# Carrying one stream of weight halves through the time mixer, the pool projections and the merge

## The chip, the core and the metric

The kernel runs on one core of a Trainium2 chip. The metric is the device time of one execution in microseconds (us), from three runs of the kernel before. The engines are TensorE (PE, with its weight loads PEld), VectorE (DVE), ScalarE (ACT), GpSimd (POOL) and SyncE (SP, which here issues transfers).

## What is computed

One decoder block: a layer norm over 272 tokens (16 of them prepended), two token mixers side by side, a gated merge, an output projection with layer norm, and a mixture of 16,384 experts with layer norm. The part that the change touches, cut from the reference:

```python
p = h @ w_in                                   # h: 272 x 2048; columns: r, k, v, low-rank parts, pool, two gates
ya = rwkv7_branch(p_rwkv, ...)                 # time mixer: 16 head pairs, delta rule over the tokens
yb = pool_branch(p_pool, w_pool, pool_scale)   # 4 groups of 256 columns, causal means over 2, 4, 8, 16 tokens minus the token,
                                               # then a 256 x 256 product per group
gate = sigmoid(p_gate + b_gate)
merged = gate[0] * (ya @ w_branch_a) + gate[1] * (yb @ w_branch_b)
h = layer_norm(ALPHA * h + merged @ w_out, ...)
h = layer_norm(ALPHA * h + peer_ffn(h, ...), ...)
```

Products that need float32 accuracy are made of three fp32r products: each operand is split into leading bits ("high") and the difference ("rest"), and high x high, high x rest and rest x high are added in PSUM.

## The kernel before

The stages run one behind the other, each in a block of its own that all engines leave together: input, low-rank projections, time mixer (rwkv_stage), pool_stage, merge_stage, out_stage, and the expert stage.

**Weights.** A weight tile of 128 columns has 16 k-tiles of 128 rows and comes in two halves of 8 k-tiles (128 x 1024 floats, 512 KB). A half is loaded by SP, its high part is made by a copy to fp32r, its rest by a subtraction on VectorE, and TensorE then does 24 products with it (8 k-tiles, three products each, in `product`, line 128).

**Time mixer.** 16 head pairs p go through a software pipeline of steps b = -1 to 18, written out by hand in ORDER: each entry is a name and an index, and STAGE gives by how many steps an entry lags (p = b - stage). `schedule` walks the list for every engine and calls that engine's function of the name where 0 <= p < 16. Entry "f" n does the next n k-tiles of the projections r, k, v of pair b on TensorE; "e" i moves a projected tile from PSUM (ScalarE line 597, then VectorE line 689); "sp" u and "ahead" round half u on ScalarE (line 586) and subtract on VectorE (line 113 through `rest_bits`). There are 48 "f" k-tiles in a step. Stage 1 (kn, lw, la, lg, ex, nm, bo, ab) makes decays, norms and keys, stage 2 (gr, rb, rk, Z, W, t) inverts the chunk matrices, stage 3 (r, u, s, yc, gm, gv, ge) runs the chain over five chunks and the group norm. So steps 16, 17 and 18 empty the pipeline: 16 has stages 1 to 3, 17 has stages 2 and 3, 18 has stage 3 alone, and none of them has an "f". "ge" on VectorE ends a pair: reciprocal (line 787), scale, bonus, and the product with the gate into `yaT` (line 794, semaphore `done`). Then "e" 2 follows, then the next step's first entries: "sp" 1, "cv", and "gr", where VectorE masks the Gram products (LT_st, line 732), on which TensorE's "rb" waits.

**Pool stage.** Four groups; SP loads 1 MB halves of 256 columns into one raw buffer (line 864) and the four 256 x 256 matrices `pool_mix` (line 867). VectorE makes high and rest of each (lines 108 and 113). TensorE does the projections `pool_u`, ScalarE copies them, VectorE adds shifted copies up to the window with a copy back after each doubling (lines 921 to 931), TensorE multiplies by `pool_mix` in plain float32 (line 876), ScalarE and VectorE make ybT_high and ybT.

**Merge stage.** 16 column tiles m, seven halves each: two gates, branch a (two halves each) and branch b (one half). Two buffers each for raw, high and rest. VectorE makes high (line 108) and rest (line 113); SP loads a half as soon as the split of the half two before it is done. At the start VectorE also splits all of `yaT` (128 x 4096). ScalarE does the sigmoids, VectorE the products, the sum and its split (`finish`, `keep`). The first and the last pass are written out, the others are a loop of the hardware over pairs of tiles. The first two transfers of `w_out` start after the first pass's loads.

Of the kernel before, what the change touches and what calls it, by code (L numbers as in the profile page):

```python
# [75 lines left out]
class Core:  # L76
# [5 lines left out]
    def sem(self, name):  # L82
        s = self.nc.alloc_semaphore(name)
        self.sems.append(s)
        return s
# [10 lines left out]
    def ps(self, name, shape, ctx):  # L96
        return ctx.enter_context(self.nc.psum_tensor(name, shape, F32))

# [168 lines left out]
def lora_stage(k, w):  # L267

    nc = k.nc
    with ExitStack() as ctx:  # L270
# [29 lines left out]
        def _(act):  # L300
# [24 lines left out]
         "r": 3, "u": 3, "s": 3, "yc": 3, "gm": 3, "gv": 3, "ge": 3}  # L325


def rwkv_stage(k, w):

    nc = k.nc  # L330
    with ExitStack() as ctx:
# [5 lines left out]
        raw = three("w_in", [P, HK, P])  # L337
        wh, wt = three("w_in_high", [P, HK, P]), three("w_in_rest", [P, HK, P])
# [26 lines left out]
        names = ("w_in0", "w_in1", "w_in2", "high", "split", "lora_w", "project", "own", "shifted", "rm", "lora_mm", "sig", "csum", "exps",  # L365
# [3 lines left out]
                 "done", "zero", "rst")  # L369
# [36 lines left out]
        W = w["w_in"][0].rearrange("(k p) c -> p k c", p=P)  # L406
# [5 lines left out]
        def _(sp):  # L412
            for b in range(PAIRS):
                for u in range(6):
                    wait(sp, q["split"], b * 6 + u - 2)
                    sp.dma_start(raw[u % 3][:], W[:, u % 2 * HK:u % 2 * HK + HK, b * P + u // 2 * D:b * P + u // 2 * D + P]).then_inc(q[f"w_in{u % 3}"], 16)
# [12 lines left out]
        def _(pe):  # L429
            at = [0]  # L430

            def f(n, b, par):

                for _ in range(n):
                    i, kt = divmod(at[0], KT)
                    u, kh = divmod(at[0], HK)
                    if kt == 0:
                        wait(pe, q["shifted"], b * 3 + i - 1)
                    if kh == 0:
                        wait(pe, q["split"], b * 6 + u + 1)  # L440
                    mm = product(nc, pr[(3 * par + i) % 2][:, 0:T], (wh[u % 3][:, kh, :], wt[u % 3][:, kh, :]),
                                 (k.hT_high[:, kt, :], k.hT[:, kt, :]), kt == 0, kt == KT - 1)
                    if kh == HK - 1:
                        mm.then_inc(q["project"], 1)
                    at[0] = (at[0] + 1) % (3 * KT)
# [135 lines left out]
        def _(act):  # L581
            def sp_(u, b, par):

                wait(act, q["project"], b * 6 + u - 2)
                wait(act, q[f"w_in{u % 3}"], b * 32 + 16 * (u // 3) + 16)
                nc.scalar.copy(wh[u % 3][:].bitcast(F32R), raw[u % 3][:]).then_inc(q["high"], 1)  # L586

            def e(i, p, par):

                o = (V_OMR, V_OMK, V_OMV)[i]  # L590
# [5 lines left out]
                wait(act, q["project"], p * 6 + 2 * i + 2)  # L596
                nc.scalar.activation(t[:, real], pr[(3 * par + i) % 2][:, 0:T], ACT.Copy, scale=cur[par][:, o:o + 1]).then_inc(q["own"], 1)
# [65 lines left out]
            def gv(_, p, par):  # L663
# [3 lines left out]

            wait(act, q["zero"], n_zero)
            schedule({"ahead": sp_, "sp": sp_, "e": e, "kn": kn_, "lw": lw, "la": la, "lg": lg, "ex": ex, "nm": nm, "ab": ab, "t": t, "r": r_, "u": u_,
                      "yc": y, "gm": gm, "gv": gv})  # L670

        @block.vector
        def _(dve):
            d, n = nc.vector.drain, nc.vector

            def sp_(u, b, par):

                wait(dve, q["high"], b * 6 + u + 1)
                rest_bits(nc.vector, wt[u % 3][:], raw[u % 3][:], wh[u % 3][:]).then_inc(q["split"], 1)
# [5 lines left out]
            def e(i, p, par):  # L685
                m = (V_MUR, V_MUK, V_MUV)[i]
                t = (r, kx, v)[i][par][:, PAD + 1:]
                wait(dve, q["own"], p * 3 + i + 1)
                n.scalar_tensor_tensor(out=t, in0=pr[(3 * par + i) % 2][:, 0:T - 1], scalar=cur[par][:, m:m + 1], in1=t,
# [95 lines left out]
            def ge(_, p, par):  # L785
# [8 lines left out]
                n.tensor_tensor(k.yaT[:, p, :], yc[:], gate[p % 3][:], ALU.mult).then_inc(q["done"], 1)  # L794
# [3 lines left out]
                      "Z": Z, "W": W_, "r": r_, "s": s_, "gm": gm, "ge": ge})  # L798
# [39 lines left out]
def pool_stage(k, w):  # L838

    nc = k.nc  # L840
    groups, gd = len(POOL_WINDOWS), POOL_DIM // len(POOL_WINDOWS)
    gt = gd // P
    with ExitStack() as ctx:
        HK = KT // 2
        raw = k.sb("pool_weights", [P, KT, gd], ctx=ctx)
        wh, wt = ([k.sb(f"pool_weights{n}{i}", [P, KT, gd], ctx=ctx) for i in range(2)] for n in ("_high", "_rest"))
        wm = k.sb("pool_mix", [P, groups, gt, gd], ctx=ctx)
        uu = k.sb("pool_in", [P, 2, gt, T], ctx=ctx)
        sm = k.sb("pool_sums", [P, 2, gt, T], ctx=ctx)
        pd = k.sb("pooled", [P, 2, gt, SEQ], ctx=ctx)  # L850
        pu = [[k.ps(f"pool_u{i}{j}", [P, 512], ctx) for j in range(gt)] for i in range(2)]
        pm = [[k.ps(f"pool_m{i}{j}", [P, 512], ctx) for j in range(gt)] for i in range(2)]
        s_w, s_wm = [k.sem("pool_w0"), k.sem("pool_w1")], k.sem("pool_wm")
        s_split, s_rest = k.sem("pool_split"), k.sem("pool_rest")
        s_u, s_uc, s_pd, s_m, s_y = k.sem("pool_u"), k.sem("pool_uc"), k.sem("pool_d"), k.sem("pool_m"), k.sem("pool_y")
        src = w["w_in"][0].rearrange("(k p) c -> p k c", p=P)
        block = ctx.enter_context(nc.Block())

        @block.sync
        def _(sp):  # L860
            for g in range(groups):
                for h in range(2):
                    wait(sp, s_split, 2 * (g - 1) + h + 1)
                    sp.dma_start(raw[:, h * HK:(h + 1) * HK], src[:, h * HK:(h + 1) * HK, POOL0 + g * gd:POOL0 + (g + 1) * gd]).then_inc(s_w[h], 16)
                if g == 0:
                    for h in range(groups):
                        sp.dma_start(wm[:, h, :, :], w["w_pool"][0, h].rearrange("(j p) d -> p j d", p=P)).then_inc(s_wm, 16)

        @block.tensor
        def _(pe):  # L870
            def mix(g):
                wait(pe, s_pd, g + 1)
                wait(pe, s_rest, gt * (g - 1))
                for j in range(gt):
                    for i in range(gt):
                        mm = nc.tensor.matmul(pm[g % 2][j][:, 0:SEQ], wm[:, g, i, j * P:(j + 1) * P], pd[:, g % 2, i, :],
                                              start=(i == 0), stop=(i == gt - 1))
                    mm.then_inc(s_m, 1)

            for g in range(groups):  # L880
                wait(pe, s_uc, gt * (g - 1))
                for j in range(gt):
                    for kt in range(KT):
                        if j == 0 and kt % HK == 0:
                            wait(pe, s_split, 2 * g + kt // HK + 1)
                        mm = product(nc, pu[g % 2][j][:, 0:T], [x[g % 2][:, kt, j * P:(j + 1) * P] for x in (wh, wt)],
# [725 lines left out]
```

## Time and profile before

| | us |
|---|---|
| three runs, median (lowest to highest) | 2838.03 (2835.0 to 2839.47) |
| the profiled execution: its time | 2838.6 |
| its span, first to last instruction | 2836.2 |
| time mixer, steps 16 to 18 (TensorE's part) | 80.7 |
| pool stage | 76.7 |
| merge stage | 369.7 |

Of the span TensorE is busy 81%, VectorE 59%, ScalarE 16%. The expert stage after 1400 us is bound by its gathers and doesn't depend on when it starts. All times within the trace count from the first instruction. A busy TensorE is not a TensorE at its peak: its products are pipelined and each record is longer than the distance to the next one.

### The profile page before, as it was taken

Reading aid. Unit: us, or ns where it says so; the run is one execution under the profiler, and the core shown is the slowest. Engines: PE = TensorE matmul, PEld = TensorE weight load, DVE = VectorE, ACT = ScalarE, POOL = GpSimd, SP = SyncE. Lnnn points to the kernel's source line nnn. Section 1 sums busy time; section 2 is a strip of 40 time slices with the busy share of each in tenths; the row PEclk is TensorE's granted clock in tenths of the full one; section 3 lists DMA queues with packets and bytes.
Section 4 is the critical chain, followed back from the end, with each engine's and each line's share of the span. In section 5 each row is a group of like instructions: output and inputs, shape, how many; then the busy total and the mean of one; then the engine's idle time right before and its main releaser. Section 6 shows DMA issues by size and latency. Waiting matters only on the chain.

```text
span 2836.2 us, 42516 instructions
## 1 busy us (share of the span) xinstructions
PE 2286.5 (81%) x17604; PEld 1614.7 (57%) x17604; DVE 1668.3 (59%) x2643; ACT 459.0 (16%) x1043; POOL 654.1 (23%) x541
## 2 busy tenths in 40 slices
PE   4899998989867799999778778878777777777776
PEld 3788888888857799997663334433223223222222
DVE  6466666666655666666655565456644634444444
ACT  1443343334320000000010111011100100000000
POOL 1000000000000000000035335435554535444442
PEclk9999999999988899999889889889999999999999
DMA  3532323232104556564479999989999999999996
GB/s 123 134 82 72 81 66 83 64 83 69 49 2 134 155 165 169 166 167 156 153 259 407 376 376 407 403 347 420 420 420 420 421 384 410 420 420 420 420 420 272
DMA packets 354342, 710.17 MB, mean 250 GB/s; under 512 B 13656, under 2 KB 278256, under 8 KB 287600
## 3 DMA queue, kind: packets, MB, share of 16 engines
q0 software_dynamic: 74176, 537.01, 46.0%
q1 hardware_dynamic: 280000, 170.78, 21.1%
q8 instruction: 124, 2.03, 0.3%
q14 instruction: 42, 0.34, 0.0%
HBM read 705.64 MB, written 2.10 MB: 250 GB/s over the span
## 4 chain that ended last, share of the span: by engine, by line
DMA 27%; PE 13%; DVE 6%; issue 2%; DVEq 1%; POOL 1%; ACT 0%; ACTq 0%
DMA down_rows<-in_v_table,experts 22%; PE peer_sum L1358 6%; DMA up_rows<-in_u_table,experts 5%; PE query_then_peer_sum L1358 5%; PE query_then_peer_sum L1321 2%; DVE up_rows L1495 2%; POOL down_rows L1303 0%; POOL up_rows L1296 0%; DVE expert_sides L1477 0%; DVE side_index L1439 0%; DVE side_index L1446 0%; DVE one_hot L1475 0%; DVE scores_left L1440 0%; DVE top_pos L1446 0%; DVE top_pos L1439 0%
## 5 line engine op out<-in xcount | busy, mean ns | idle before, releaser
L1495 DVE CUSTOM_DVE_ANT_0 up_rows<-up_rows,h 128x2048 f32<-128x2048 f32 x256 | 585.5, 2292 | 624.6 <-DMA up_rows<-in_u_table,experts 624.6
L1296 POOL DMA_INDIRECT up_rows<-in_u_table,experts x256 | 271.6, 1061 | 1463.6 <-DVE experts L1481 1370.9
L1358 PE MATMUL query_then_peer_sum<-down_rows,diagonal 128*128 128x512 f32 x1024 | 472.9, 607 | 157.5 <-DMA down_rows<-in_v_table,experts 108.7
L1358 PE MATMUL peer_sum<-down_rows,diagonal 128*128 128x512 f32 x1024 | 476.0, 608 | 98.6 <-DMA down_rows<-in_v_table,experts 95.0
L1303 POOL DMA_INDIRECT down_rows<-in_v_table,experts x256 | 374.0, 1461 | 613.9 <-PE peer_sum L1358 316.5
L1358 PEld LDWEIGHTS query_then_peer_sum<-down_rows,diagonal 128*128 128x128 f32 x1024 | 186.3, 191 | 444.0 <-DMA down_rows<-in_v_table,experts 240.0
L1358 PEld LDWEIGHTS peer_sum<-down_rows,diagonal 128*128 128x128 f32 x1024 | 191.3, 193 | 340.2 <-issue 188.4
L128 PE MATMUL project<-hT_high,w_in_high 128*128 128x272 f32 x768 | 246.1, 320 | 11.1 <-DVE w_in_rest L113 11.1
L128 PE MATMUL project<-hT_high,w_in_rest 128*128 128x272 f32 x768 | 223.0, 290 | 0.0
L128 PE MATMUL project<-hT,w_in_high 128*128 128x272 f32 x768 | 222.4, 290 | 0.0
L1415 ACT ACTIVATE dots<-dots 128x4 f32<-128x4 f32 x64 | 13.1, 205 | 997.4 <-DVE dots L1495 997.4
L113 DVE TENSOR_TENSOR w_in_rest<-w_in,w_in_high 128x1024 fp32r<-128x1024 f32 x96 | 117.2, 1220 | 91.4 <-ACT w_in_high L586 91.4
L128 PE MATMUL merge_ps<-hT_high,merge_w_high 128*128 128x256 f32 x512 | 152.0, 297 | 22.9 <-DVE merge_w_rest L113 21.9
L128 PEld LDWEIGHTS project<-hT_high,w_in_high 128*128 128x128 f32 x768 | 145.8, 190 | 17.1 <-DVE w_in_rest L113 11.3
L128 PEld LDWEIGHTS project<-hT,w_in_high 128*128 128x128 f32 x768 | 146.1, 190 | 3.8
L128 PE MATMUL merge_ps<-hT,merge_w_high 128*128 128x256 f32 x512 | 146.2, 285 | 0.0
L128 PE MATMUL merge_ps<-hT_high,merge_w_rest 128*128 128x256 f32 x512 | 146.1, 285 | 0.0
L128 PEld LDWEIGHTS project<-hT_high,w_in_rest 128*128 128x128 f32 x768 | 145.8, 190 | 0.0
L113 DVE TENSOR_TENSOR merge_w_rest<-merge_w,merge_w_high 128x1024 fp32r<-128x1024 f32 x112 | 137.3, 1226 | 8.3
L108 DVE CAST merge_w_high<-merge_w 128x1024 fp32r<-128x1024 f32 x112 | 77.6, 693 | 102.5 <-DMA merge_w<-in_w_in 46.5
L128 PEld LDWEIGHTS merge_ps<-hT_high,merge_w_high 128*128 128x128 f32 x512 | 99.3, 194 | 33.3 <-DVE merge_w_rest L113 32.8
L586 ACT CAST w_in_high<-w_in 128x1024 fp32r<-128x1024 f32 x96 | 100.1, 1043 | 10.5 <-DMA w_in<-in_w_in 6.0
(308 smaller groups left out, 3665.7 us busy)
## 6 DMA issues: line engine op xcount, KB each, us to landing
w_in<-in_w_in SPq DMA_DIRECT2D x96, 512.0 KB, 4.4
merge_w<-in_w_in SPq DMA_DIRECT2D x64, 512.0 KB, 4.0
merge_w<-in_w_branch_a SPq DMA_DIRECT2D x32, 512.0 KB, 3.9
out_w<-in_w_out SPq DMA_DIRECT2D x16, 1024.0 KB, 5.1
pool_weights<-in_w_in SPq DMA_DIRECT2D x8, 1024.0 KB, 5.4
merge_w<-in_w_branch_b SPq DMA_DIRECT2D x16, 512.0 KB, 3.9
out_w<-in_w_q_peer SPq DMA_DIRECT2D x8, 1024.0 KB, 17.4
query_w<-in_w_q_peer SPq DMA_DIRECT2D x8, 1024.0 KB, 28.2
```

The costliest lines, as they stand in the source:

```text
L108: return nc.vector.tensor_copy(high.bitcast(F32R), x)
L113: return eng.tensor_tensor(low.bitcast(F32R), x, high, ALU.subtract)
L128: mm = nc.tensor.matmul(out, a.bitcast(F32R), b.bitcast(F32R), start=start and n == 0, stop=stop and n == 2)
L586: nc.scalar.copy(wh[u % 3][:].bitcast(F32R), raw[u % 3][:]).then_inc(q["high"], 1)
L1296: pool.indirect_dma_start(ur[n % RU][:], None, w["u_table"][0], bass.IndirectOffsetOnAxis(ap=k.idx[:, t, h, j:j + 1], axis=0)).then_inc(s_ ...
L1303: pool.indirect_dma_start(vr[n % RV][:], None, w["v_table"][0], bass.IndirectOffsetOnAxis(ap=k.idx[:, t, h, j:j + 1], axis=0)).then_inc(s_ ...
L1321: mm = nc.tensor.matmul(pq[i][:, 0:SEQ], wt[h % 2][i][:, kt, :], k.h1T[:, kt, :], start=(kt == 0), stop=(kt == KT - 1))
L1358: mm = nc.tensor.matmul(acc[t][c][:], dg[n % RD][:], vr[n % RV][:, c * 512:(c + 1) * 512], start=False, stop=(n % (HEADS * TOPK) == HEADS ...
L1415: nc.scalar.activation(x, x, ACT.Gelu).then_inc(s_gelu, 1)
L1495: v.tensor_tensor_reduce(ur[n % RU][:], ur[n % RU][:], k.h[:, n // (HEADS * TOPK), :], 1.0, 0.0, ALU.mult, ALU.add, dots[:, n:n + 1]).then ...
```

## The change

A list `halves` holds all weight halves of the time mixer (96), of the pool projections (16) and of the merge (112) in the order of use. Three raw, three high and three rest buffers carry it, with semaphores that live through both stages. `load_half`, `round_half` (ScalarE) and `rest_half` (VectorE) treat every half alike. Pool projections: the "f" entries of steps 16 to 18 do the eight pool tiles (128 k-tiles: 48, 48 and 32), "e" copies them on VectorE into `pool_in`. The last entries of step 18 round the first three merge halves. "ge" leaves y in `yc`; ScalarE copies it into `ya_high`, and a new entry "gy" at the end of the list subtracts on VectorE into `ya_rest`, so that the split of all of `yaT` is gone. `pool_stage` is gone: its window sums (without the copies back) stand in the first two slots of VectorE's merge, its mix between the gate products and the branch a product of tile m = 0. The merge is fully written out, with rounding on ScalarE.

Its core:

```diff
+    def load_half(self, sp, g):
+        src, h, c0 = self.halves[g]
+        wait(sp, self.s_split, g - 2)
+        sp.dma_start(self.w_raw[g % 3][:], src[:, h * KT // 2:(h + 1) * KT // 2, c0:c0 + P]).then_inc(self.s_raw[g % 3], 16)
+
+    def round_half(self, act, g):
+        wait(act, self.s_used, g - 2)
+        act.wait_ge(self.s_raw[g % 3], 16 * (g // 3) + 16)
+        self.nc.scalar.copy(self.w_high[g % 3][:].bitcast(F32R), self.w_raw[g % 3][:]).then_inc(self.s_rounded, 1)
+
+    def rest_half(self, dve, g):
+        dve.wait_ge(self.s_rounded, g + 1)
+        rest_bits(self.nc.vector, self.w_rest[g % 3][:], self.w_raw[g % 3][:], self.w_high[g % 3][:]).then_inc(self.s_split, 1)
...
-    ("ab", 0), ("W", 5), ("gm", 0), ("f", 4), ("gv", 0), ("f", 4), ("ge", 0), ("e", 2),
+    ("ab", 0), ("W", 5), ("gm", 0), ("f", 4), ("gv", 0), ("f", 4), ("ge", 0), ("e", 2), ("gy", 0),
...
+STREAM = ("ahead", "sp", "f", "e")
...
-                    if name in units and 0 <= p < PAIRS:
+                    if name in units and 0 <= p < (PAIRS + 4 if name in STREAM else PAIRS):
...   # SP, end of the time mixer
+            for g in range(PAIRS * 6, k.merge_at + 3):
+                k.load_half(sp, g)
...   # VectorE, "e"
+                if p >= PAIRS:
+                    if tile < k.merge_at // 2:
+                        dve.wait_ge(k.s_used, 2 * tile + 2)
+                        n.tensor_copy(k.pool_in[:, tile - 3 * PAIRS, :], pr[tile % 2][:, 0:T]).then_inc(q["shifted"], 1)
+                    return
...   # ScalarE, between "gv" and "e" 2
+            def ge(_, p, par):
+                wait(act, q["y"], p + 1)
+                nc.scalar.copy(k.ya_high[:, p, :].bitcast(F32R), yc[:]).then_inc(q["yhigh"], 1)
...   # VectorE
-                n.tensor_tensor(k.yaT[:, p, :], yc[:], gate[p % 3][:], ALU.mult).then_inc(q["done"], 1)
+                n.tensor_tensor(yc[:], yc[:], gate[p % 3][:], ALU.mult).then_inc(q["y"], 1)
+            def gy(_, p, par):
+                wait(dve, q["yhigh"], p + 1)
+                rest_bits(n, k.ya_rest[:, p, :], yc[:], k.ya_high[:, p, :]).then_inc(q["done"], 1)
...   # merge_stage, SP
+            for g in range(groups):
+                sp.dma_start(wm[:, g, :, :], w["w_pool"][0, g].rearrange("(j p) d -> p j d", p=P)).then_inc(s_wm, 16)
+            for g in range(first + 3, last):
+                k.load_half(sp, g)
+                if g == first + 12:
...   # the two w_out transfers
...   # merge_stage, TensorE
+            for m in range(KT):
+                wait(pe, s_done, m - 1)
+                if m == 1:
+                    pe.wait_ge(s_yb, 2 * groups)
+                tile(m, 0, h)
+                tile(m, 1, h)
+                if m == 0:
+                    mix()
+                tile(m, 2, (k.ya_high, k.ya_rest))
+                if m == 0:
+                    pe.wait_ge(s_yb, 2 * groups)
+                tile(m, 3, (k.ybT_high, k.ybT))
...   # merge_stage, VectorE
+            for m in range(KT):
+                for j, (n, h) in enumerate(parts):
+                    g = first + m * PARTS + j
+                    if g + 3 < last:
+                        k.rest_half(dve, g + 3)
+                    if j == 0 and m:
+                        keep(m - 1)
+                    if m == 0 and j < 2:
+                        window(2 * j)
+                        window(2 * j + 1)
```

In the merge ScalarE's list is likewise: round half g + 3 at slot g, then at fixed slots the sigmoids, the copy of the last sum into `mT_high`, and (m = 0, slot 3) the eight copies into `ybT_high`.

## Rows read from the trace of the kernel before

**Rows 1.** Windows by stage: length; PE, PEld, DVE, ACT, POOL busy; clock; DMA

```profile
725.88:770.52 44.64, 41.43 (x702) 38.42 (x701) 30.23 (x61) 17.08 (x35) 0.00 (x0) 1.00 0.11 31
770.52:804.05 33.53, 24.85 (x557) 20.43 (x556) 22.59 (x52) 10.77 (x27) 0.00 (x0) 0.93 0.01 2
804.05:828.93 24.88, 20.04 (x545) 18.12 (x545) 15.25 (x37) 4.78 (x16) 0.00 (x0) 0.95 0.01 3
828.93:851.20 22.27, 12.60 (x140) 9.01 (x140) 8.67 (x17) 3.39 (x13) 0.00 (x0) 0.53 0.00 1
851.20:927.90 76.70, 60.10 (x416) 57.87 (x416) 43.51 (x45) 6.89 (x16) 0.00 (x0) 0.86 0.41 124
927.90:1297.60 369.70, 344.89 (x2688) 329.76 (x2688) 251.10 (x325) 15.61 (x33) 0.00 (x0) 0.97 0.59 165
```

**Rows 2.** Timeline of VectorE: the same instruction of steps 4 and 15

```profile
224.92 0.17 DVE L730 COPY chunk_decay<-decay_prod 128x5 f32<-128x5 f32 x1
730.16 0.17 DVE L730 COPY chunk_decay<-decay_prod 128x5 f32<-128x5 f32 x1
```

**Rows 3.** Timeline, step 14 into 15: start, us, engine, line, operation, idle before it

```profile
725.99 0.49 ACT L597 ACTIVATE v<-project,pair_vectors 128x272 f32<-128x272 f32 x1 [0.98 <-PE project L128]
726.38 1.03 ACT L586 CAST w_in_high<-w_in 128x1024 fp32r<-128x1024 f32 x1
...
728.01 0.43 DVE L794 TENSOR_TENSOR yaT<-y,gate 128x256 f32<-128x256 f32 x1
728.35 0.49 DVE L689 SCALAR_TENSOR_TENSOR v<-project,pair_vectors,v 128x271 f32<-128x271 f32 x1
728.76 1.22 DVE L113 TENSOR_TENSOR w_in_rest<-w_in,w_in_high 128x1024 fp32r<-128x1024 f32 x1
...
730.23 0.49 DVE L732 TENSOR_TENSOR LT_st<-invert,constants 128x320 f32<-128x320 f32 x1
...
731.45 0.63 PE L387 MATMUL invert<-R_st,B_st 64*64 64x64 f32 x16
```

**Rows 4.** Timeline of TensorE: six k-tiles of projection to what follows; a chain wait

```profile
728.83 0.39 PE L128 MATMUL project<-hT_high,w_in_high 128*128 128x272 f32 x1
...
731.29 0.33 PE L387 MATMUL chain<-rhs,Y_st 64*64 64x64 f32 x4
...
836.93 0.48 PE L387 MATMUL chain<-BKV_by_token 64*64 64x64 f32 x4 [0.31 <-ACT U L652]
```

**Rows 5.** Tile pool_sums, one line of it: count, ns min/median/max, first and last

```profile
L925 DVE TENSOR_TENSOR pool_tmp<-pool_sums x6: 695/715/721, 890.4 to 920.7; 128x538 f32<-128x538 f32 x3, 128x530 f32<-128x530 f32 x2, 128x514 f32<-128x514 f32 x1
```

**Rows 6.** Timeline: start of the pool stage on SP, its end and the merge's start on TensorE

```profile
852.40 1.01 SPq L864 DMA_DIRECT2D pool_weights<-in_w_in  x2
853.46 4.30 SPq L867 DMA_DIRECT2D pool_mix<-in_w_pool  x4
...
923.08 3.78 PE L876 MATMUL pool_m<-pooled,pool_mix 128*128 128x256 f32 x8 [4.51 <-DVE pooled L931]
...
935.27 0.41 PE L128 MATMUL merge_ps<-hT_high,merge_w_high 128*128 128x256 f32 x1
...
939.12 0.41 PE L128 MATMUL merge_ps<-hT_high,merge_w_high 128*128 128x256 f32 x1
```

**Rows 7.** Tile merge_w_high; transfers with us to landing; two matmuls nine apart

```profile
L108 DVE CAST merge_w_high<-merge_w x112: 683/694/696, 932.4 to 1292.3; 128x1024 fp32r<-128x1024 f32 x112
L113 DVE TENSOR_TENSOR merge_w_rest<-merge_w,merge_w_high x112: 1224/1226/1228, 933.2 to 1293.0; 128x1024 fp32r<-128x1024 f32 x112
...
merge_w<-in_w_in SPq DMA_DIRECT2D x64, 512.0 KB, 4.0
...
pool_mix<-in_w_pool SPq DMA_DIRECT2D x4, 256.0 KB, 7.1
...
1107.19 0.28 PE L128 MATMUL merge_ps<-hT_high,merge_w_high 128*128 128x256 f32 x1
1108.25 0.28 PE L128 MATMUL merge_ps<-hT_high,merge_w_high 128*128 128x256 f32 x1
```

More of the change, by code:

```diff
@@ L676, in sp_ @@
             def sp_(u, b, par):
-                wait(dve, q["high"], b * 6 + u + 1)
-                rest_bits(nc.vector, wt[u % 3][:], raw[u % 3][:], wh[u % 3][:]).then_inc(q["split"], 1)
+                if b * 6 + u < k.merge_at + 3:
+                    k.rest_half(dve, b * 6 + u)
             def cv(_, p, par):
@@ L835, in row_broadcast, with merge_stage, mixed @@
     return v.rearrange("(a d) -> a d", a=1).to_broadcast((P, D))
-def pool_stage(k, w):
+def merge_stage(k, w):
     nc = k.nc
-    groups, gd = len(POOL_WINDOWS), POOL_DIM // len(POOL_WINDOWS)
-    gt = gd // P
+    groups = len(POOL_WINDOWS)
     with ExitStack() as ctx:
         HK = KT // 2
[L845 to L856, printed above, removed]
+        parts = [(n, h) for n, kts in enumerate((KT, KT, KT, KT // 2)) for h in range(kts // HK)]
+        PARTS = len(parts)
+        gt = [k.sb(f"merge_gates{i}", [P, 2, SEQ], ctx=ctx) for i in range(2)]
+        ps = [[k.ps(f"merge_ps{i}{n}", [P, 512], ctx) for n in range(4)] for i in range(2)]
+        wm, sums = k.pool_mix, k.pool_sums
+        s_wm, s_pd, s_mix = k.sem("pool_wm"), k.sem("pool_d"), k.sem("pool_mixed")
+        s_yb_high, s_yb = k.sem("pool_y_high"), k.sem("pool_y")
+        s_gate, s_sum, s_high, s_done = k.sem("merge_gate"), k.sem("merge_sum"), k.sem("merge_high"), k.sem("merge_done")
+        first, last = k.merge_at, k.merge_at + KT * PARTS
         block = ctx.enter_context(nc.Block())
+        def mixed(m):
+            return ps[1][m // 2][:, m % 2 * SEQ:m % 2 * SEQ + SEQ]
         @block.sync
@@ L869, in _ @@
+            for g in range(first + 3, last):
+                k.load_half(sp, g)
+                if g == first + 12:
+                    for i in range(2):
+                        sp.dma_start(k.out_raw[i][:], w["w_out"][0].rearrange("(k p) c -> p k c", p=P)[:, 4 * i:4 * i + 4, 0:512]).then_inc(k.s_out_w[i], 16)
         @block.tensor
         def _(pe):
[L871 to L886, printed above, removed]
-                                     (k.hT_high[:, kt, :], k.hT[:, kt, :]), kt == 0, kt == KT - 1)
-                    mm.then_inc(s_u, 1)
-                if g == 1:
-                    pe.wait_ge(s_wm, 16 * groups)
-                if g:
-                    mix(g - 1)
@@ L893, in _, with tile @@
-            mix(groups - 1)
+            def tile(m, n, xs):
+                hs = [j for j, (o, _) in enumerate(parts) if o == n]
+                for j in hs:
+                    g = first + m * PARTS + j
+                    pe.wait_ge(k.s_split, g + 1)
+                    for kh in range(HK):
+                        kt = parts[j][1] * HK + kh
+                        mm = product(nc, ps[m % 2][n][:, 0:SEQ], [x[g % 3][:, kh, :] for x in (k.w_high, k.w_rest)],
+                                     [x[:, kt, :] for x in xs], kt == 0, j == hs[-1] and kh == HK - 1)
+                    mm.then_inc(k.s_used, 1)
@@ new lines, in mix @@
+            def mix():
+                pe.wait_ge(s_wm, 16 * groups)
+                for g in range(groups):
+                    pe.wait_ge(s_pd, g + 1)
+                    for j in range(2):
+                        for i in range(2):
+                            mm = nc.tensor.matmul(mixed(2 * g + j), wm[:, g, i, j * P:(j + 1) * P], k.pool_in[:, 2 * g + i, META:T],
+                                                  start=(i == 0), stop=(i == 1))
+                        mm.then_inc(s_mix, 1)
@@ L1093, in out_stage @@
+            keep(KT - 1)
 def out_stage(k, w):
@@ L1573, in program @@
                 lora_stage(k, w)
+            k.open_weights(w, front)
+            k.ya_high, k.ya_rest = (k.sb(f"yaT_{n}", [P, KT, SEQ], ctx=front) for n in ("high", "rest"))
+            k.pool_in = k.sb("pool_in", [P, POOL_DIM // P, T], ctx=front)
             rwkv_stage(k, w)
```

301 lines of the change are left out of this document (99 added, 202 removed).

## The prediction, made before the change was run

> **What bounds the kernel now.** I read the windows by stage first [rows 1]. Their rows are the last full step of the time mixer (15), the emptying steps 16, 17 and 18, the pool stage and the merge, cut where TensorE starts each. In the full step TensorE is busy 41.43 of 44.64 us at full clock: it sets the pace. In the emptying steps it is busy 24.85 of 33.53, 20.04 of 24.88 and 12.60 of 22.27 us, the last at a granted clock of 0.53, near the lower of its two levels (1.2 and 2.4 GHz). There it waits for VectorE and ScalarE, and that time is free for other products. The pool stage is 76.70 us with 60.10 of TensorE. The merge is 369.70 us. Its work is 112 halves of 24 products; between two products of an undisturbed run lie (1108.25 - 1107.19) / 9 = 0.118 us [rows 7], so 2.83 us a half and 317 us in all. The other 53 us are waits and low clock, since two buffers make load, split and use wait for each other. Then I read single instructions in the timeline: the end of a step [rows 3], a chain wait [rows 4], and both ends of the pool stage [rows 6]. The stages before the time mixer and after the merge keep their work, and the expert stage moves as a whole with the end of the merge, so the sum covers the time from step 4 to the end of the merge.
>
> **The ends of the full steps (A).** New: ScalarE copies y into ya_high and VectorE subtracts (gy). The copy sits on ScalarE ahead of "e" 2 and "sp" 1, and waits for VectorE's product with the gate, which ends at 728.44; before, ScalarE did "e" 2 at 725.99 and the rounding at 726.38 [rows 3]. Queued behind that wait are "e" 2 (0.49), the rounding (1.03), and the next copies of the chain. The copy has no row; I take 0.4, between 0 and the 0.49 of "e" 2, which is longer by 16 columns. So "e" 2 ends on ScalarE near 729.25, on VectorE near 729.75 (before: 728.84), gy (as long as the 0.43 of line 794) near 730.1, the rounding near 730.2, its subtraction (1.22) near 731.45 instead of 729.98. Everything behind on VectorE is late by 1.45 us, LT_st too: it ends at 732.2 instead of 730.72. TensorE's "rb" waits for it and began at 731.45, so 0.7 of the 1.45 was slack, and 0.75 us is lost. Behind that, TensorE's own order covers VectorE's delay. Bounds: 0 (slack elsewhere) and 1.5 (all of it passes on). Twelve steps' ends (3 to 14) lie ahead of step 15: 12 x 0.75 = **+9.0** (0 to 18).
>
> **Steps 15 and 16 (B).** Step 16 now holds three pool tiles and is a full step again; its "e" is one VectorE copy instead of two moves, which I value at -0.2. A full step takes (730.16 - 224.92) / 11 = 45.93 us [rows 2]. New: 2 x (45.93 + 0.75) - 0.2 = 93.2; before 44.64 + 33.53 = 78.17. **+15.0.**
>
> **Step 17 (C).** Three more tiles. Six k-tiles take 731.29 - 728.83 = 2.46 us with their start [rows 4], four of them 1.70 by share of products. A step has six runs of 6 and three of 4: 19.86. With 20.04 us of other work that is 39.9 if every gap is filled and 44.7 if none is. In step 16 the same sum with all gaps filled is 24.85 + 19.86 = 44.7, and the measured full step has 1.2 more. Step 17 lacks the decays and norms that keep VectorE late, so I take half of that, and 0.75 for the end of step 16: 41.25 against 24.88, **+16.4** (15 to 20).
>
> **Step 18 (D).** Two tiles: five runs of 6 (12.3) and one of 2 (0.95). The runs stand between u and s of the chain and cover ScalarE's copy of U, 0.31 in each of five chunks [rows 4], so -1.55. With products between, the clock should stay up: of 12.60 us at the low level, some 8 lie ahead of the tail (the mean and variance products and their waits) and would take half: -4. The new copy and subtraction end the stage: +0.9. 22.27 + 13.25 - 1.55 - 4 + 0.9 = 30.9, **+8.6** (4 to 13, without cover and clock, or with S covered too). The roundings and subtractions of these steps are hidden under the runs; without that cover each costs 1.03 + 1.22.
>
> The time mixer ends 49 us later. **Pool stage:** -76.7.
>
> **Start of the merge (E).** From the time mixer's end at 851.20 to the first transfer behind it 1.2 us pass [rows 6], and stay. Three halves lie ready. The clock is low: 18 products take 939.12 - 935.27 = 3.85, so the first half takes 5.1, the next two 2.85 each: 10.8. The fourth, half 115, stands on SP behind the four loads of pool_mix, which took 4.30 to issue; with 4.0 to landing [rows 7], rounding and subtraction it is ready near 11.6. TensorE does it until 14.5. VectorE has done its subtraction at 11.6 and then does the window sums, which nothing hides: 1 + 2 + 3 + 4 additions and 4 combinations of some 0.72 [rows 5], 10.1, with the gaps between them I say 11 us, and the subtraction of 116 between them: 23.7. TensorE stands until then, its last mix at low clock takes 3.8 [rows 6], which gives 27.5 with the first groups' mix done in the wait. Then halves 116 (partly at low clock, 4.7), 117 and 118: **38 us** for m = 0 (31, if transfers and windows come earlier, to 44).
>
> **The other 15 tiles (F).** Rounding on ScalarE 1.03, subtraction 1.23, issue and landing about 4.4: 6.7 us for a raw buffer that comes round every three halves (8.6 us), and 2.3 us for a high buffer that is given back two halves before its next use is due. VectorE has 7 x 1.23 = 8.6 us of it a tile and ScalarE 7 x 1.03 = 7.2, with a few operations of 256 columns each, both not much over half of the 20 us. So TensorE is the bound: 2.83 + 0.04 for a half's first product (a guess), 105 x 2.87 = **301.4**. Upper bound: the old pace, 369.70 / 112 = 3.30 a half. A rule speaks against moving the rounding. VectorE rounded a half in 0.69 [rows 7] where ScalarE takes 1.03 [rows 3]. The Trainium skill ("ScalarE: Activation LUTs", Rules for kernel authors) wants simple elementwise work on VectorE, which it gives up to three times ScalarE's rate in bf16; the rows show 1.5 times here. By the rows the longer rounding lies under 5.7 us of other halves' products.
>
> **Sum.** Before, from 851.20 to the merge's end: 76.7 + 369.7 = 446.4. After, from the same point: 9.0 + 15.0 + 16.4 + 8.6 + 1.2 + 38 + 301.4 = 389.6. Gain 56.8, so 2838.6 - 56.8 = 2781.8 against the profiled execution, which stands 0.6 above the median of three runs; I say **2781**.
>
> **Rivals.** (1) VectorE's whole delay passes on at each of 14 ends of steps: 14 x 0.75 = 10.5 more, 2791.5. For it: TensorE waits for VectorE at several other places in a step. Against: it follows its own order for some 5 us behind "rb". (2) The ends of steps cost nothing and the runs fill every gap: A and B lose 10.5, C 1.4, D 4.6, so 2765. For it: step 16 shows how near filling comes. (3) The merge keeps its pace, that is, three buffers do not free TensorE: 105 x (3.30 - 2.87) = 45 more, 2826. Against: its waits begin with split and load, which get one more buffer. (4) Slower than before: the weights themselves. The raw ring gives one half per (0.4 + landing + 1.03 + 1.23) / 3. At a landing of 5.9 us it reaches TensorE's 2.87; the gain of 57 is gone at 3.41 a half, a landing of 7.6; at 8 us it is 3.55, 72 more, 2853. For it: pool_mix landed in 7.1 with several transfers queued [rows 7]. Against: 4.0 for the very transfers, at a DMA share of 0.59 [rows 1], which a pace of 2.87 lifts to about 0.68. (5) The rounding lies on the path: 112 x 0.34 = 38 more, 2820. It needs TensorE to use up its two ready halves. The rule on ScalarE above would make this the outcome; the trace so far speaks against it.
>
> **How the numbers follow.** Chances: the forecast 0.64, with its own range 2765 to 2797; rival 1 0.12, 2 0.10, 3 0.07, 4 0.04, 5 0.03. The range 2762 to 2804 takes in the forecast's, 1 and 2, and leaves out 3, 4 and 5 and some of the forecast's tails, about 2 in 10. A measurement of this kernel can tell about 0.2%, 5.7 us, from no change: only rival 4 isn't faster by that, and a landing between 7 and 7.6 us would be within. So faster 0.95, same 0.01, slower 0.04.
>
> **What would show it.** The copies of chunk_decay 46.7 us apart instead of 45.9 would bear out A, with a new wait of TensorE's "rb" for LT_st near 0.75. Step 17 near 41 and step 18 near 31 us at a clock above 0.8 bear out C and D. In the merge's first tile: a wait of some 9 us before the last mix. From the second tile on TensorE's windows at 2.87 a half with no waits for the subtraction; waits of ScalarE's rounding for a transfer would be rival 4. The prediction is wrong if projections in the emptying steps open new waits in the chain, or if the merge's pace isn't TensorE's.

## The result, and the profile after

| | before | after |
|---|---|---|
| median of 4 runs each, us | 2836.52 (2832.26 to 2839.47) | 2772.14 (2770.33 to 2773.89) |
| ratio, 95% interval | | 0.9774 [0.9757, 0.9791] |
| profiled execution, us (span) | 2838.6 (2836.2) | 2773.89 (2771.8) |
| end of the time mixer, us from the start | 851.20 | 900.18 |
| end of the merge | 1297.60 | 1235.2 |

The kernel became 64.4 us faster; the forecast was a gain of 56.8 and a time of 2781, in a range that holds the measured one. Run once more (k9_changed below), the same two kernels stood at 2773.72 and 2830.90, a gain of 57.2. So several us of a single difference belong to the run, and the steps below are read from traces, not from the totals.

The windows of the changed kernel, by stage, as [rows 1] has them for the kernel before (length; busy time of TensorE, its weight loads, VectorE, ScalarE, GpSimd; granted clock; DMA share; GB/s). They are step 17, step 18, the merge's start with its first tile, and its other 15 tiles:

```profile
828.36:867.00 38.64, 38.49 (x695) 36.34 (x695) 24.55 (x47) 10.30 (x22) 0.00 (x0) 1.00 0.31 84
867.00:900.20 33.20, 22.24 (x232) 19.01 (x230) 16.40 (x28) 9.68 (x21) 0.00 (x0) 0.88 0.18 48
900.20:935.40 35.20, 29.94 (x202) 28.24 (x203) 20.49 (x29) 11.56 (x18) 0.00 (x0) 0.92 0.56 150
935.40:1235.20 299.80, 299.80 (x2520) 299.75 (x2518) 147.67 (x163) 123.81 (x148) 0.00 (x0) 1.00 0.68 185
```

In the last row TensorE is busy all the time, at full clock: the merge has become TensorE's. In the row of step 17 it is busy 38.49 of 38.64 us, where step 17 of before stood for 4.84 of 24.88 [rows 1].

The waits in that last stretch (who waited, for whom: us in total, times, longest):

```profile
ACT w_half_high L124 <- PE merge_ps L160: 160.0, 97, 1.8
DVE w_half_rest L145 <- ACT w_half_high L124: 145.6, 103, 4.7
ACT w_half_high L124 <- DMA w_half<-in_w_in: 5.5, 4, 2.6
```

None of the waits in this stretch is TensorE's. ScalarE waits 97 times for TensorE to give a rounded buffer back, and only a few times for a transfer: the data are there before their place is.

The end of step 14 into 15, timeline of VectorE, ScalarE and TensorE (start, us, engine, line, operation, idle before it), to be laid beside [rows 3]:

```profile
737.56 0.43 DVE L837 TENSOR_TENSOR y<-y,gate 128x256 f32<-128x256 f32 x1
738.02 0.41 ACT L704 CAST yaT_high<-y 128x256 fp32r<-128x256 f32 x1 [3.46 <-DVE y L837]
738.33 0.48 ACT L631 ACTIVATE v<-project,pair_vectors 128x272 f32<-128x272 f32 x1
738.84 0.50 DVE L732 SCALAR_TENSOR_TENSOR v<-project,pair_vectors,v 128x271 f32<-128x271 f32 x1 [0.86 <-ACT v L631]
739.26 0.41 DVE L145 TENSOR_TENSOR yaT_rest<-y,yaT_high 128x256 fp32r<-128x256 f32 x1
739.78 1.23 DVE L145 TENSOR_TENSOR w_half_rest<-w_half,w_half_high 128x1024 fp32r<-128x1024 f32 x1
741.26 0.48 DVE L775 TENSOR_TENSOR LT_st<-invert,constants 128x320 f32<-128x320 f32 x1
741.89 0.68 PE L419 MATMUL invert<-R_st,B_st 64*64 64x64 f32 x16 [0.72 <-DVE LT_st L775]
```

ScalarE's copy stands ahead of its part of v, and waits 3.46 us for VectorE's product with the gate; v's second half on VectorE then waits 0.86 for ScalarE, and TensorE's R_st x B_st 0.72 for `LT_st`. Before, the same product followed without a wait [rows 3].

The same VectorE instruction of steps 4 and 15, as in [rows 2]:

```profile
226.84 0.16 DVE L773 COPY chunk_decay<-decay_prod 128x5 f32<-128x5 f32 x1
...
741.19 0.16 DVE L773 COPY chunk_decay<-decay_prod 128x5 f32<-128x5 f32 x1
```

Eleven steps take 514.35 us, 46.76 a step against 45.93.

Step 18, first chunk of the chain (timeline of ScalarE and TensorE):

```profile
868.96 0.40 ACT L704 CAST yaT_high<-y 128x256 fp32r<-128x256 f32 x1 [3.44 <-DVE y L837]
869.27 1.04 ACT L124 CAST w_half_high<-w_half 128x1024 fp32r<-128x1024 f32 x1
870.22 0.20 ACT L682 COPY rhs<-chain 128x64 f32<-128x64 f32 x1
870.48 0.33 PE L419 MATMUL chain<-rhs,Y_st 64*64 64x64 f32 x4 [1.30 <-ACT rhs L682]
871.54 0.33 PE L419 MATMUL chain<-BKV_by_token 64*64 64x64 f32 x4 [0.73 <-ACT U L686]
```

The chain's copy of `rhs` stands behind the copy of y and a rounding on ScalarE, and TensorE waits 1.30 and then 0.73 us.

The merge's start (SP, ScalarE, VectorE, TensorE), as [rows 6] for before:

```profile
901.49 3.34 SPq L910 DMA_DIRECT2D pool_mix<-in_w_pool  x4
910.15 1.05 ACT L124 CAST w_half_high<-w_half 128x1024 fp32r<-128x1024 f32 x1 [10.44 <-DMA w_half<-in_w_in]
912.51 0.39 PE L160 MATMUL merge_ps<-hT_high,w_half_high 128*128 128x256 f32 x1 [0.24 <-DVE w_half_rest L145]
915.43 3.62 PE L936 MATMUL merge_ps<-pool_in,pool_mix 128*128 128x256 f32 x16
920.80 1.99 PE L936 MATMUL merge_ps<-pool_in,pool_mix 128*128 128x256 f32 x8 [1.75 <-DVE pool_in L991]
923.98 0.69 DVE L991 SCALAR_TENSOR_TENSOR pool_in<-pool_sums,pool_in 128x512 f32<-128x512 f32 x1
924.73 1.99 PE L936 MATMUL merge_ps<-pool_in,pool_mix 128*128 128x256 f32 x8 [1.94 <-DVE pool_in L991]
```

### The profile page after: what moved, and what is told of

The parts are those of the page before. It is cut to its first block, busy times and chain, and to the rows that moved or that the text cites. A ratio compares the mean times of both kernels' runs of the same rounds, so it can differ in the third digit from the quotient of the medians.

```text
span 2771.8 us, 41744 instructions
## 1 busy us (share of the span) xinstructions
PE 2258.8 (81%) x17604; PEld 1602.2 (58%) x17604; DVE 1574.3 (57%) x2507; ACT 592.0 (21%) x1195; POOL 653.6 (24%) x541
## 4 chain that ended last, share of the span: by engine, by line
DMA 28%; PE 14%; DVE 6%; issue 2%; DVEq 1%; POOL 1%; ACT 0%; ACTq 0%
DMA down_rows<-in_v_table,experts 22%; PE peer_sum L1291 7%; DMA up_rows<-in_u_table,experts 5%; PE query_then_peer_sum L1291 5%; PE query_then_peer_sum L1254 2%; DVE up_rows L1428 2%; POOL down_rows L1236 0%; DVE expert_sides L1410 0%; POOL up_rows L1229 0%; DVE side_index L1379 0%; DVE side_index L1372 0%; DVE one_hot L1408 0%; DVE scores_left L1373 0%; DVE top_pos L1379 0%; DVE top_pos L1372 0%
## 5 line engine op out<-in xcount | busy, mean ns | idle before, releaser
L145 DVE TENSOR_TENSOR w_half_rest<-w_half,w_half_high 128x1024 fp32r<-128x1024 f32 x224 | 273.8, 1223 | 270.8 <-ACT w_half_high L124 269.4
L160 PE MATMUL project<-hT_high,w_half_high 128*128 128x272 f32 x896 | 286.9, 320 | 11.2 <-DVE w_half_rest L145 11.2
L124 ACT CAST w_half_high<-w_half 128x1024 fp32r<-128x1024 f32 x224 | 234.4, 1047 | 197.2 <-PE merge_ps L160 163.9
L160 PE MATMUL project<-hT_high,w_half_rest 128*128 128x272 f32 x896 | 260.4, 291 | 0.0
L160 PE MATMUL project<-hT,w_half_high 128*128 128x272 f32 x896 | 259.9, 290 | 0.0
L160 PEld LDWEIGHTS project<-hT_high,w_half_high 128*128 128x128 f32 x896 | 170.5, 190 | 18.6 <-DVE w_half_rest L145 11.4
L160 PEld LDWEIGHTS project<-hT,w_half_high 128*128 128x128 f32 x896 | 170.6, 190 | 4.1
L160 PEld LDWEIGHTS project<-hT_high,w_half_rest 128*128 128x128 f32 x896 | 170.4, 190 | 0.0
L160 PE MATMUL merge_ps<-hT,w_half_high 128*128 128x256 f32 x512 | 145.1, 283 | 0.0
L160 PE MATMUL merge_ps<-hT_high,w_half_rest 128*128 128x256 f32 x512 | 144.9, 283 | 0.0
## 6 DMA issues: line engine op xcount, KB each, us to landing
out_w<-in_w_q_peer SPq DMA_DIRECT2D x8, 1024.0 KB, 18.1
```

The costliest lines, as they stand in the source:

```text
L124: self.nc.scalar.copy(self.w_high[g % 3][:].bitcast(F32R), self.w_raw[g % 3][:]).then_inc(self.s_rounded, 1)
L145: return eng.tensor_tensor(low.bitcast(F32R), x, high, ALU.subtract)
L160: mm = nc.tensor.matmul(out, a.bitcast(F32R), b.bitcast(F32R), start=start and n == 0, stop=stop and n == 2)
```

## The experiments

My theory: the gain is what the pool tiles find free in the emptying steps, plus a merge that a third raw buffer makes TensorE's; the losses are the new copy at each step's end and the windows that stand open in the merge's first tile. The rivals are that another part of the change freed the merge (the third rounded buffer, or the rounding's move to ScalarE), and that the pool tiles' place is indifferent.

**Two raw buffers in the merge.** The load of a half waits for the split of the half two before it, not three before it as in the changed kernel, so that only two of the three raw buffers are in use.

```diff
-        wait(sp, self.s_split, g - 2)
+        wait(sp, self.s_split, g - 1 if g >= self.merge_at + 3 else g - 2)
```

> From half 115 on (the merge) a load waits one split longer, so that two raw buffers are in flight instead of three; high and rest keep three. Theory (the merge's old pace was set by the ring of raw buffers: load, round, subtract, with only two of them): a half then takes (0.4 issue + 4.0 landing + 1.05 rounding + 1.23 subtraction + hand-overs) / 2 = 3.35 to 3.4 us instead of 2.86, so the merge is some 55 us longer and the kernel near 2825; ScalarE's rounding waits for transfers in the trace. Rival (the pace came from the high and rest buffers, or from VectorE's rounding, and the third raw buffer adds nothing): 2772, within 5.

Measured: 2821.42 us, ratio to the kernel before 0.9962 [0.9946, 0.9978]. From the start of the first `ybT` half (931.9) to the end of the last (1286.3) lie 106 halves in 354.4 us, 3.34 us each; in the changed kernel the same takes 302.8, 2.857 each. The waits from 940 to 1280:

```profile
ACT w_half_high L124 <- DMA w_half<-in_w_in: 118.9, 56, 4.2
ACT w_half_high L124 <- DMA w_half<-in_w_branch_a: 59.0, 30, 4.4
...
PE merge_ps L160 <- DVE w_half_rest L145: 34.2, 51, 2.8
```

ScalarE now waits 178 us for those two transfers alone, and TensorE for the subtraction. With a landing of 4.1 us in this run, (0.4 + 4.1 + 1.05 + 1.23) / 2 = 3.39 us a half, close to the 3.34: the ring of loads sets the pace. The third raw buffer is worth 52 us of the changed kernel's merge; without it the kernel is 10.9 us faster than before.

The sum holds for the kernel before too: its 106 halves took 339.6 us (958.0 to 1297.6), 3.20 each, and with VectorE's 0.69 for the rounding (0.4 + 4.0 + 0.69 + 1.23) / 2 = 3.16. With two raw buffers the slower rounding on ScalarE thus made the ring slower, not faster. This kernel keeps the written-out merge and has no split of all of `yaT` either, so neither of these freed the merge.

**Two rounded buffers in the merge.** Rounding and subtraction of half g + 2 stand at slot g, and the rounding waits for the use of half g.

```diff
-        wait(act, self.s_used, g - 2)
+        wait(act, self.s_used, g - 1 if g >= self.merge_at + 3 else g - 2)
...
-                    if g + 3 < last:
-                        k.round_half(act, g + 3)
+                    if first + 3 <= g + 2 < last:
+                        k.round_half(act, g + 2)
```

(the same for the subtraction on VectorE)

> In the merge the rounding of a half comes one slot later and waits for the use of the half two before it, so that high and rest have two buffers in use; raw keeps three. Theory (only the raw ring set the old pace): after a half's use 1.05 + 1.23 and hand-overs are 2.4 us, under the 2.86 that TensorE spends on the half in between, so the pace stays at 2.86 and the time within 5 us of 2772, with at most some tenths of a us a tile where VectorE's products delay a subtraction. Rival (the third high and rest buffer frees TensorE): back to 3.1 to 3.3 a half, 2797 to 2820.

Measured: 2771.07 us, ratio 0.9783 [0.9767, 0.9800]. The part behind the first tile takes 305.1 us, 2.3 more than in the changed kernel; the first tile is 3 shorter, since VectorE comes to the windows sooner. The third rounded buffer gains next to nothing: it did not free the merge.

**VectorE rounds in the merge**, all three buffers as in the changed kernel.

```diff
-                    if g + 3 < last:
-                        k.round_half(act, g + 3)
...
-                        k.rest_half(dve, g + 3)
+                        x = (g + 3) % 3
+                        dve.wait_ge(k.s_used, g + 1)
+                        dve.wait_ge(k.s_raw[x], 16 * ((g + 3) // 3) + 16)
+                        split(nc, k.w_high[x][:], k.w_rest[x][:], k.w_raw[x][:]).then_inc(k.s_split, 1)
```

> In the merge VectorE rounds and subtracts, as before the change, with the stream's three buffers of each kind; ScalarE rounds only up to half 114. Theory (TensorE is the bound, whoever rounds): VectorE needs 7 x (0.69 + 1.23 + 0.08) + 1.7 = 15.7 us of the 20 a tile, so the pace stays at 2.86; the first tile may lose 1 to 3 us, since VectorE has the window sums there too: 2772 to 2776. Rival (moving the rounding to ScalarE was what freed the merge): 3.1 to 3.3 a half, 2797 to 2820. The rule that simple elementwise work belongs on VectorE would have it faster: 2765 or less.

Measured: 2777.76 us, ratio 0.9806 [0.9790, 0.9823], some us above what I expected, though the intervals of this ratio and the changed kernel's overlap. Its first tile is 2.9 us longer and the part behind it 303.8, 1.0 longer. Its waits:

```profile
DVE w_half_high L140 <- PE merge_ps L160: 60.5, 81, 0.9
DVE w_half_high L140 <- DMA w_half<-in_w_branch_b: 5.2, 1, 5.2
```

VectorE, too, waits for TensorE to give buffers back and not for data. With three raw buffers it hardly matters where the rounding stands; its move did not free the merge.

**The pool tiles behind step 18.** The projections of the eight pool tiles leave the emptying steps and run in one piece behind them.

```diff
-                        if name in units and 0 <= p < (PAIRS + 4 if name in STREAM else PAIRS):
+                        if name in units and 0 <= p < PAIRS:
...
+            f(POOL_DIM // P * KT, PAIRS, 0)
```

(and rounding, subtraction and the moves likewise in one run on their engines)

> The eight pool tiles stand behind step 18 in one run instead of in the runs of steps 16 to 18; the stream, its order and its buffers are the same. Theory (the emptying steps' gaps cover a part of the projections, and the rest of the pool stage's saving is the stream's: no load to wait for, no separate mix): steps 16 to 18 go back to some 81 us plus the new ends of steps, and the projections take 16 x 3.0 + 2.3 for the first split + 2.5 of low clock = 53 in a row, so the time mixer's end moves from 900 to some 918 and the kernel to 2790 (2786 to 2794). Rival (the cover is the whole gain of the part): 2772 + 40 or more.

Measured: 2793.49 us, ratio 0.9862 [0.9842, 0.9882]. The run of pool tiles:

```profile
867.30:923.50 56.20, 50.41 (x384) 50.22 (x384) 26.86 (x28) 19.38 (x19) 0.00 (x0) 0.95 0.56 150
```

It takes 56.2 us up to the merge's first product, where the pool stage of before took 76.70 [rows 1]: the stream of halves is loaded ahead, and the windows and the mix stand in the merge now, where they still take time. The merge's first product comes at 923.5 instead of 901.5: in the emptying steps the same tiles cost 22 us less, the free time of TensorE there. So the place of the tiles counts, and both rivals fall, mine and that the cover is the whole gain of the part.

**The copy of y later.** ScalarE's copy of y goes behind the key norms of the next step, VectorE's subtraction behind the second Z product; the list runs one step longer for the last pair, and nothing else moves.

```diff
-    ... ("t", 1), ("kn", 0), ("f", 6),
-    ("r", 1), ("Z", 1), ("u", 1), ("lw", 0), ...
+    ... ("t", 1), ("kn", 0), ("gc", 0), ("f", 6),
+    ("r", 1), ("Z", 1), ("u", 1), ("gy", 0), ("lw", 0), ...
-    ... ("ge", 0), ("e", 2), ("gy", 0),
+    ... ("ge", 0), ("e", 2),
-         ... "ge": 3, "gy": 3}
+         ... "ge": 3, "gc": 4, "gy": 4}
```

> ScalarE's copy of y into its high part and VectorE's subtraction leave the end of the step and stand in the next one: the copy behind the key norms, the subtraction behind the second Z product, where both engines wait. Theory (the copy holds up ScalarE's move of v, its rounding and so VectorE's masks, and TensorE's product R_st x B_st waits 0.72 us for them in every step): the wait is gone, copies of chunk_decay lie 45.8 to 46.0 us apart again instead of 46.7, 13 steps x 0.75 = 9.8 less, and up to 2 us in step 18 where the chain's first copies stood behind it: 2760 to 2763. Rival (any place costs its VectorE and ScalarE time): 2768 to 2772.

Measured: 2757.67 us, ratio 0.9740 [0.9726, 0.9755]. The two marks of [rows 2], and R_st x B_st of step 15:

```profile
227.44 0.16 DVE L773 COPY chunk_decay<-decay_prod 128x5 f32<-128x5 f32 x1
...
731.55 0.17 DVE L773 COPY chunk_decay<-decay_prod 128x5 f32<-128x5 f32 x1
...
732.85 0.63 PE L419 MATMUL invert<-R_st,B_st 64*64 64x64 f32 x16
```

45.83 us a step: the old pace, and the wait of R_st x B_st is gone. The merge starts at 888.4 instead of 901.5. The place of the copy and its subtraction had cost 13 us, a little more than I expected: from the start of step 18 to the merge's first product it takes 31.9 us (856.5 to 888.4) for 35.2 in the changed kernel, and of the waits of 1.30 and 0.73 us in the chain's first chunk only one of 0.31 is left.

**The copy of y behind v.** ScalarE moves its part of v first, then copies y; the rest stays.

```diff
-    ... ("ge", 0), ("e", 2), ("gy", 0),
+    ... ("ge", 0), ("e", 2), ("gc", 0), ("gy", 0),
```

> ScalarE moves v (e 2) first and copies y behind it; the subtraction stays at the step's end. Theory (the delay of VectorE's masks is the sum of what stands ahead of them: 0.92 from v behind the copy, the rest from the subtraction and the rounding behind the copy): the masks come 1.1 us late instead of 1.45, of which 0.7 is slack, so TensorE's wait for LT_st falls from 0.72 to 0.3 to 0.45 and the steps are 46.3 us: 2767. Rival (the copy's wait itself is what holds the step): 0.72 stays, 46.7.

Measured: 2769.76 us, ratio 0.9784 [0.9766, 0.9802], and in the trace:

```profile
734.00 0.43 DVE L145 TENSOR_TENSOR yaT_rest<-y,yaT_high 128x256 fp32r<-128x256 f32 x1
734.96 1.23 DVE L145 TENSOR_TENSOR w_half_rest<-w_half,w_half_high 128x1024 fp32r<-128x1024 f32 x1 [0.53 <-ACT w_half_high L124]
737.06 0.68 PE L419 MATMUL invert<-R_st,B_st 64*64 64x64 f32 x16 [0.34 <-DVE LT_st L775]
```

The wait falls from 0.72 to 0.34, and a step from 46.76 to 46.43 us (510.72 / 11). So about half of it was v waiting behind the copy on ScalarE. The rest is not VectorE's subtraction of y: behind it VectorE stands another 0.53 us for the rounded half, since ScalarE's rounding still stands behind the copy. The total alone would not tell this from no change.

**The windows first.** VectorE computes three of the four groups of windows ahead of half 115's subtraction, and the fourth behind it.

```diff
+                    if g == first:
+                        for y in range(3):
+                            window(y)
                     if g + 3 < last:
                         k.rest_half(dve, g + 3)
...
-                    if m == 0 and j < 2:
-                        window(2 * j)
-                        window(2 * j + 1)
+                    if g == first:
+                        window(3)
```

> In the merge's first tile VectorE sums three windows before it waits for half 115, and the fourth behind it, instead of two and two behind halves 115 and 116. Theory (TensorE's first tile waits for VectorE's sums, 1.75 and 1.94 us ahead of the last two mixes, and mixes late): VectorE stands 11 us for that transfer now and would use 7 of them, the last sum ends 8 us earlier, the mix runs without waits behind half 115, and the first tile is 4 to 5 us shorter: 2767 to 2768. Rival (half 115 comes later or TensorE's start is set by something else): within 1 us of 2772.

Measured: 2768.22 us, ratio 0.9776 [0.9763, 0.9789]. From the merge's start to its first `ybT` half it takes 27.2 us, in the changed kernel 932.3 - 901.5 = 30.8: 3.6 less, as three of the windows now fill most of VectorE's 11.06 us of waiting for half 115. The total is not enough to show it, so both kernels ran side by side on one chip, the changed kernel and this one again:

> The changed kernel as it is, timed beside the next one on the same chip, so that a few us can be told. Every theory expects the ratio that it had, 0.976 to 0.979, and copies of chunk_decay 46.7 us apart.

> The kernel with three window sums ahead of half 115 once more, beside the changed kernel. Its first tile was 3.6 us shorter in the trace, while its ratio to the kernel before was that of the changed kernel. Theory (the first tile's end moves everything behind it): 3 to 4 us under the changed kernel of the same chip. Rival (the expert stage gives it back): within 1 us of it.

Measured: 2773.72 (0.9799 [0.9785, 0.9812]) and 2767.60 us (0.9777 [0.9764, 0.9790]). 6.1 us apart, of which the two merges account for 3.9 (332.9 and 329.0). The order of the windows is worth about 4 us by the traces; the 6 of the totals has its own spread.

**Both: the later copy and the windows first.**

> Both moves together: the copy and subtraction of y in the next step and three window sums ahead of half 115. Theory: they lie in different stages and add: 2756 to 2759, about 14 us under the changed kernel. Rival (one takes what the other gives): not below the better of the two alone.

Measured: 2753.56 us (2752.48 to 2755.40), ratio 0.9722 [0.9709, 0.9736]. The merge runs from 885.6 to 1214.9. By ratio that is about 0.5%, some 15 us, under the changed kernel. On the same chip the better of the two alone stood at 2757.67, with a ratio whose interval overlaps this one; in the traces the merge takes 329.3 us for 333.5 there, so the windows' gain comes on top.

## Why the prediction was right, step by step

Right as a whole, since the pool stage's removal and the merge's pace were read from the right rows. The sum from step 4 to the end of the merge, cut where TensorE starts a step; the time mixer ends with VectorE's last instruction, at 900.18, and so it does at the 851.20 of [rows 1], which is no start of TensorE:

| term | forecast | measured | from |
|---|---|---|---|
| A, ends of steps 3 to 14 | +9.0 | +9.6 | step 15 starts at 735.44 for 725.88 |
| B, steps 15 and 16 | 93.2 (+15.0) | 92.9 (+14.8) | 735.44 to 828.36 |
| C, step 17 | 41.25 (+16.4) | 38.0 (+13.2) | 828.36 to 866.39 |
| D, step 18 | 30.9 (+8.6) | 33.8 (+11.5) | 866.39 to 900.18 |
| E, merge's start and first tile | 39.2 | 35.0 | 900.18 to 935.19 |
| F, the other 15 tiles | 301.4 | 300.0 | 935.19 to 1235.2 |
| gain to the end of the merge | 56.8 | 62.4 | 1297.6 - 1235.2 |

**A held** with its mechanism: the wait at R_st x B_st that was forecast at 0.75 is 0.72, and steps lie 46.76 apart for 46.7. Moving the copy and its subtraction takes the wait and the whole cost away (k4_gy_later), moving it behind v halves it (k8_copy_behind_v). That VectorE's full 1.45 us passes on (rival 1) is refuted, and so is that the ends cost nothing (rival 2).

**C and D each missed, and cancelled by luck:** together 71.8 for 72.2. In C the projections were sized rightly, and what lies between them was not. The starts of step 17, before and after, and one run of six k-tiles:

```profile
804.05 1.33 PE L387 MATMUL invert<-A_st,B_st 64*64 64x64 f32 x20
806.88 0.28 PE L387 MATMUL chain<-BKV_by_token,MT_st 64*64 64x64 f32 x4
...
828.36 0.80 PE L419 MATMUL invert<-A_st,B_st 64*64 64x64 f32 x20
830.15 0.28 PE L419 MATMUL chain<-BKV_by_token,MT_st 64*64 64x64 f32 x4
...
831.30 0.39 PE L160 MATMUL project<-hT_high,w_half_high 128*128 128x272 f32 x1
833.76 0.33 PE L419 MATMUL chain<-rhs,Y_st 64*64 64x64 f32 x4
```

A run of six takes 2.46 us up to what follows, as in [rows 4], and all nine of the step 19.9 for 19.86. The other work takes 38.0 - 19.9 = 18.1 where I had taken the busy time of step 17 before, 20.04. About 1.0 of these 1.9 is the clock: its first three groups of products took 2.83 us then, at a granted clock of 0.59, and take 1.79 now. How the other 0.9 splits is not shown; busy time counts each record whole, also where the next product would have followed sooner. Nor did the 1.35 come that I had added for gaps and for the end of step 16: TensorE is busy for 38.49 of 38.64 us.

In D two things failed. One is the claim that the new copy and the roundings lie hidden under the runs. They stand on ScalarE ahead of the chain's own copies, as the lines of step 18 show: the first chunk waits 1.30 and 0.73 us where I had subtracted 0.31 a chunk. TensorE stands some 11 us in the step where my sum left 9. The other is the clock. At 0.88 over the step it came back as assumed, but not at once, and the second run of six took 3.94 us (871.92 to 875.86) where I had 2.46:

```profile
867.00:871.50 4.50, 2.51 (x22) 2.15 (x20) 3.63 (x8) 2.52 (x5) 0.00 (x0) 1.00 0.00 0
871.50:876.50 5.00, 4.77 (x34) 4.41 (x34) 1.74 (x4) 0.15 (x1) 0.00 (x0) 0.66 0.74 195
```

Behind 4.50 us with TensorE busy for 2.51, it ran the next five at a granted clock of 0.66. In k4_gy_later, with the copy and the subtraction elsewhere, both are gone: the first chunk waits 0.31 us, the clock is at 1.00 from 856.5 to 866.0, and the second run takes 2.45 (860.24 to 862.69). So the place of the copy is the cause of the two waits, and with them of the slow run. New waits in the chain were the sign that I had set for being wrong; these are not opened by the projections, but my sum had left them out. The end of the stage, 0.9 longer by the copy and the subtraction, is as forecast.

**E was over-sized by 4.2 us, by the clock.** Its order was right: half 115 comes at 912.5 and the last window ends at 924.67, 23.1 us behind the merge's start for 23.7. The 9 us that I said TensorE would stand (915.43 to 924.73) hold three groups of the mix, two in 3.62 us and one in 1.99, and so only 1.75 and 1.94 us of waiting. The clock did not fall there, it was granted at 1.00: the last mix takes 1.99 where I took the 3.78 of [rows 6], and half 116 runs at full pace where I had 4.7. That is 3.7 of the 4.2.

**F held**: 300.0 / 105 = 2.857 us a half for 2.87, no waits for the subtraction, a DMA share of 0.68 as worked out. That the merge keeps its pace (rival 3) and that landing binds (rival 4) are refuted here, and k1_raw2 shows how near the second is: the landing is 4.2 us in the changed kernel, and with a buffer less the pace goes to 3.34. Rival 5, rounding on the path, is refuted by the waits (ScalarE waits for TensorE, 160 us) and by k3_round_dve. The Trainium skill ("ScalarE: Activation LUTs", Rules for kernel authors) wants simple elementwise work on VectorE. The rates in the traces point the same way, 1.05 us on ScalarE for the 0.69 of [rows 7]; the time of this kernel does not: with the rounding on VectorE, it took 2777.76 us, no faster.

**The rest.** A to D cancel to within 0.1 us, and E and F give the 5.6 us by which the gain to the merge's end beat the forecast (4.2 + 1.4). In the profiled executions another 2 us lie behind the merge, in the expert stage, whose work is the same. Three transfers of the chain that ended last, of the kernel before:

```profile
2234.05 15.45 DMA down_rows<-in_v_table,experts
2348.14 12.63 DMA down_rows<-in_v_table,experts
2446.16 15.93 DMA down_rows<-in_v_table,experts
```

and the same three of the changed kernel:

```profile
2167.79 18.09 DMA down_rows<-in_v_table,experts
2285.93 11.22 DMA down_rows<-in_v_table,experts
2381.22 15.93 DMA down_rows<-in_v_table,experts
```

Counted from the merge's end (1297.6 and 1235.2), the changed kernel is 3.9 us ahead at the first, 0.2 behind at the second and 2.5 ahead at the third. So the 2 us are of the size by which this stage wanders in the two executions. Why it does is open; nothing ties it to the change, and the gain of 57.2 in k9_changed doesn't show it.

## What to carry to other kernels

Look first at which engine waits for what in a streamed stage: where the raw data's ring is too short, one more load buffer gives TensorE its pace (here 2.86 us a half for 3.34), while, once it is there, more rounded buffers or another engine for the rounding move almost nothing. Free time in a pipeline's emptying steps can carry the work of a later stage, but don't take the busy time of a step with waits and a lower clock for the time that its work will need between other products (here 20.04 us for 18.1), and look at the in-order engines that serve both the stream and the chain. A short new instruction costs what stands behind it on its engine: a 0.41 us copy that waits for another engine, with the subtraction behind it, cost 13 us over the mixer, and next to nothing once both were placed where their input was long ready.

## What the runs showed of the hardware that I had not expected

TensorE was busy for 299.80 of 299.80 us at a granted clock of 1.00, while the DMA engines were at a share of 0.68; at that share the 512 KB transfers landed in 4.1 to 4.2 us, hardly later than in the 4.0 at 0.59 [rows 1, 7]. The clock did not fall between the groups of the mix in the merge's first tile, with waits of 1.75 and 1.94 us around a group of 1.99; it did in step 18, where TensorE had been busy for 2.51 of 4.50 us. Why in one and not in the other is not shown.
